# An up projection of a convolved network laid out token-major, with its chunks turned through memory

## The reference, cut to what matters

```
def causal_dwconv(x, w):            # width 3, per channel, over tokens
    ...
def conv_ffn(h, w_up, conv_w, conv_b, w_down):
    u = causal_dwconv(h @ w_up, conv_w) + conv_b      # h 256x1024, w_up 1024x5632
    a, b = jnp.split(u, 2, axis=-1)                   # two halves of 2816
    return (jax.nn.silu(a) * b) @ w_down              # w_down 2816x1024
...
x = x + conv_ffn(rmsnorm(x, norm_ffn[l]), w_up[l], ffn_conv[l], ffn_conv_b[l], w_down[l])
```

## Time and profile before

| | us |
|---|---|
| median of 3 runs | 1137.87 (1137.77 to 1138.19) |
| the profiled execution | 1137.35 |
| its span | 1135.6 |
| TensorE busy | 1126.9 |
| VectorE busy | 755.1 |
| ScalarE busy | 588.0 |
| GpSimd busy | 106.9 |

### The profile page before, as it was taken

How to read it: one execution, slowest core, us unless ns; L and a number is a source line. 1 busy time by engine, 2 the same in 40 slices (tenths; PEclk the granted TensorE clock), 3 DMA queues, 4 the chain that set the end, 5 groups by cost and what they waited for, 6 DMA issues and landing times.

```text
span 1135.6 us, 16361 instructions
## 1 busy us (share of the span) xinstructions
PE 1126.9 (99%) x6345; PEld 984.8 (87%) x6345; DVE 755.1 (66%) x959; ACT 588.0 (52%) x782; POOL 106.9 (9%) x161
## 2 busy tenths in 40 slices
PE   9999999999999999999999999999999999999997
PEld 8998888888889999988888888899888888889886
DVE  6866687657776887853665664665766576655566
ACT  6664654446565766643544443564554365444453
POOL 6410311000011000000000000200500020000020
PEclk9999999999999999999999999999999999999999
DMA  8643753455644765555588766475466568776642
GB/s 259 202 159 98 227 186 115 163 202 180 216 142 132 248 214 186 182 191 183 169 280 258 236 214 205 157 224 164 142 214 216 173 196 283 252 242 223 210 140 77
DMA packets 137294, 220.30 MB, mean 194 GB/s; under 512 B 12565, under 2 KB 70026, under 8 KB 137227
## 3 DMA queue, kind: packets, MB, share of 16 engines
q1 hardware_dynamic: 133625, 209.14, 57.4%
q10 hardware_dynamic: 3506, 10.23, 2.5%
q0 software_dynamic: 96, 0.01, 0.1%
HBM read 212.91 MB, written 6.42 MB: 193 GB/s over the span
## 4 chain that ended last, share of the span: by engine, by line
PE 94%; DVE 3%; DMA 1%; issue 1%; ACT 1%; POOL 0%; POOLq 0%; DVEq 0%; ACTq 0%
PE ACCP L897 28%; PE ACCP L895 28%; PE ACCP L896 28%; PE SMP L1112 3%; DVE CONVF L2338 1%; PE SMP L1105 1%; DVE LO L2209 1%; DMA RAW<-in_w_in_dram 1%; PE SMP L1060 1%; PE SMP L1065 1%; PE SMP L1059 1%; PE SMP L1279 0%; PE SMP L1263 0%; PE SMP L1447 0%; DMA POST_GAIN<-in_ple_post_g_dram 0%
## 5 line engine op out<-in xcount | busy, mean ns | idle before, releaser
L2209 DVE TENSOR_TENSOR LO<-RAW,HI 128x1024 fp32r<-128x1024 f32 x365 | 437.7, 1237 | 210.2 <-ACT HI L1636 205.8
L1636 ACT ACTIVATE HI<-RAW 128x1024 fp32r<-128x1024 f32 x366 | 370.2, 1054 | 262.4 <-PE ACCP L897 214.0
L895 PE MATMUL ACCP<-HI,XH 128*128 128x512 f32 (+1 forms) x712 | 278.0, 391 | 0.0
L897 PE MATMUL ACCP<-HI,XL 128*128 128x512 f32 (+1 forms) x712 | 275.7, 387 | 0.0
L896 PE MATMUL ACCP<-LO,XH 128*128 128x512 f32 (+1 forms) x712 | 275.4, 387 | 0.0
L895 PE MATMUL ACCP<-XH,HI 128*128 128x256 f32 x640 | 181.7, 284 | 0.3 <-DVE CONVF L2338 0.3
L897 PE MATMUL ACCP<-XH,LO 128*128 128x256 f32 x640 | 181.1, 283 | 0.0
L896 PE MATMUL ACCP<-XL,HI 128*128 128x256 f32 x640 | 181.1, 283 | 0.0
L897 PEld LDWEIGHTS ACCP<-HI,XL 128*128 128x128 f32 x712 | 133.7, 188 | 27.3
L896 PEld LDWEIGHTS ACCP<-LO,XH 128*128 128x128 f32 x712 | 133.8, 188 | 26.4
L895 PEld LDWEIGHTS ACCP<-HI,XH 128*128 128x128 f32 x712 | 133.8, 188 | 26.2
(11 more groups left out here) (405 smaller groups left out, 1134.7 us busy)
## 6 DMA issues: line engine op xcount, KB each, us to landing
RAW<-in_w_in_dram SPq DMA_DIRECT2D x104, 512.0 KB, 4.5
RAW<-in_w_up_dram SPq DMA_DIRECT2D x44, 512.0 KB, 4.5
RAW<-in_ffn_w_gate_dram SPq DMA_DIRECT2D x44, 512.0 KB, 4.7
RAW<-in_ffn_w_up_dram SPq DMA_DIRECT2D x44, 512.0 KB, 4.6
RAW<-in_ffn_w_down_dram SPq DMA_DIRECT2D x44, 512.0 KB, 4.3
RAW<-in_w_down_dram SPq DMA_DIRECT2D x22, 512.0 KB, 4.1
scratch_hidden<-TURNED SPq DMA_DIRECT2D x20, 256.0 KB, 5.4
BLOCKS<-scratch_hidden SPq DMA_DIRECT2D x80, 64.0 KB, 2.4
```

Source lines behind the costliest of these rows:

```text
L895: pe.matmul(dst, lhs[0], rhs[0], start=start, stop=False)
L897: return pe.matmul(dst, lhs[1], rhs[0], start=False, stop=stop)
L1636: act.activation(HI[:, n % RING, half_of(half)], RAW[:, n % RAWS, half, :], ACT.Copy).then_inc(hi_ready, 1)
L2209: dve.tensor_tensor(LO[:, s, c], RAW[:, n % RAWS, half, :], HI[:, s, c].bitcast(f32), ALU.subtract).then_inc(lo_ready[s], 1)
```

## The change: what it does

The up projection gets the layout of ffn1 and ffn2. Its first 20 blocks become ten token-major rounds of two blocks (r even: 512 features of half a, r odd: 512 of half b), in five chunks; the last two blocks (256 features of each half) stay feature-major. `f_open`, OPENED and the twelve transposes go. A round's two banks are turned in 32x32 blocks by VectorE straight out of ACCP (`up_turn`), stored to memory in one transfer and read back in four (`up_moves`, placed behind the loads 2r + 7 and 2r + 8). ScalarE then (`up_take`) copies the round to PLAIN and writes the last tap with bias to UA or UB; VectorE adds the two other taps from PLAIN (`chunk_taps`, eight instructions a round). Silu is one instruction of 128x1024 a chunk; the product of a chunk is one GpSimd instruction of 128x1024; the splits HH and HL are one instruction each a chunk. Of the blocks that are prepared behind each chunk's second block, LO's second half is made by GpSimd. The rest tiles keep the old path (`rest_base`, `rest_conv`). The hardware loops of this phase are written out. In ffn1 and ffn2, `hidden_out` becomes one store instead of two and `hidden_in` four reads instead of eight, with both token tiles in each.

```diff
-T_OPEN = {"mix_v": 4, "ple_g": 4, "ffn1": 4, "ffn2": 4}
-F_OPEN = {"up": 3}
+T_OPEN = {"up": 4, "mix_v": 4, "ple_g": 4, "ffn1": 4, "ffn2": 4}
+HALF_ON_POOL = tuple(FIRST["up"] + 4 * c + 1 + RING for c in range(GLU_CHUNKS))
+WIDE = ("up",) + GLUS
-        elif phase in GLUS:
+        elif phase in WIDE:
...
-        UA = at("UA", 44, [P, 2, 2, SEQ])
-        UB = at("UB", 48, [P, 2, 2, SEQ])
+        UA = at("UA", 44, [P, 4, SEQ])
+        UB = [at("UB0", 48, [P, 4, SEQ]), at("UB1", 76, [P, 4, SEQ])]
+        PLAIN = at("PLAIN", 56, [P, 4, SEQ])
+        UP_TURNED = [at(f"UP_TURNED{i}", 60 + 4 * i, [P, 4, NT, 4, 32]) for i in range(2)]
+        UP_BLOCKS = [at(f"UP_BLOCKS{i}", 68 + 4 * i, [P, 4, NT, 4, 32]) for i in range(2)]
+        UP_REST = [at(f"UP_REST{i}", 80 + 2 * i, [P, 2, SEQ]) for i in range(2)]
+        up_rows = [nc.dram_tensor(f"scratch_up{i}", (4, 32, 4, NT * 128), f32) for i in range(2)]
         UAT, UBT = at("UAT", 44, [P, NT, 512]), at("UBT", 48, [P, NT, 512])
-        TURNED, BLOCKS = at("TURNED", 62, [P, NT, 4, 4, 32]), at("BLOCKS", 66, [P, NT, 4, 4, 32])
-        hidden_rows = nc.dram_tensor("scratch_hidden", (NT, 4, 32, 4, 128), f32)
+        TURNED, BLOCKS = at("TURNED", 62, [P, 4, NT, 4, 32]), at("BLOCKS", 66, [P, 4, NT, 4, 32])
+        hidden_rows = nc.dram_tensor("scratch_hidden", (4, 32, 4, NT * 128), f32)
...
-                for m in range(NT):
-                    sp.wait_ge(turned, NT * n + m + 1)
-                    wait(sp, blocks_in, 64 * NT * n)
-                    sp.dma_start(hidden_rows[m].rearrange("b f r c -> (b f) r c"), TURNED[:, m].rearrange("p r k t -> p r (k t)")).then_inc(turned_out, 16)
+                sp.wait_ge(turned, NT * (n + 1))
+                wait(sp, blocks_in, 64 * n)
+                sp.dma_start(hidden_rows[:, :, :, :].rearrange("b f r c -> (b f) (r c)"), TURNED[:, :, :, :, :].rearrange("p r m k t -> p (r m k t)")).then_inc(turned_out, 16)
             def hidden_in(phase, c):
                 n = chunks_before(phase, c)
-                sp.wait_ge(turned_out, 16 * NT * (n + 1))
+                sp.wait_ge(turned_out, 16 * (n + 1))
                 wait(sp, blocks_split, NT * n)
-                for m in range(NT):
-                    for r in range(4):
-                        sp.dma_start(BLOCKS[32 * r:32 * r + 32, m].rearrange("p b k t -> p b (k t)"),
-                                     hidden_rows[m, :, :, r, :].rearrange("b f c -> f b c")).then_inc(blocks_in, 16)
+                for r in range(4):
+                    sp.dma_start(BLOCKS[32 * r:32 * r + 32].rearrange("p b m k t -> p b (m k t)"),
+                                 hidden_rows[:, :, r, :].rearrange("b f c -> f b c")).then_inc(blocks_in, 16)
...
+            def up_moves(loaded):
+                for r in range(2 * GLU_CHUNKS):
+                    if loaded == 2 * r + 7:
+                        for m in range(NT):
+                            acc_is_taken(sp, "up", Turn(r), m)
+                        wait(sp, up_in[r % 2], 64 * (r // 2))
+                        sp.dma_start(up_rows[r % 2][:, :, :, :].rearrange("b f r c -> (b f) (r c)"),
+                                     UP_TURNED[r % 2][:, :, :, :, :].rearrange("p r m k t -> p (r m k t)")).then_inc(up_out[r % 2], 16)
+                    if loaded == 2 * r + 8:
+                        sp.wait_ge(up_out[r % 2], 16 * (r // 2 + 1))
+                        wait(sp, up_base, r - 1)
+                        for q in range(4):
+                            sp.dma_start(UP_BLOCKS[r % 2][32 * q:32 * q + 32].rearrange("p b m k t -> p b (m k t)"),
+                                         up_rows[r % 2][:, :, q, :].rearrange("b f c -> f b c")).then_inc(up_in[r % 2], 16)
+            def load_up():
+                for j in range(GLU_T):
+                    q = j // 2
+                    load("up", Turn(j), t_block(w["w_up"], (q % 2) * DFF + 512 * (q // 2), j % 2))
+                    up_moves(j)
+                for i in range(2):
+                    load("up", Turn(GLU_T + i), f_block(w["w_up"], i * DFF + 512 * GLU_CHUNKS))
+                    up_moves(GLU_T + i)
+                for j in range(COUNT["down"]):
+                    load("down", Turn(j), d_block(w["w_down"], j))
+                    up_moves(GLU_T + 2 + j)
...
-            norm_roots("norm_ffn", "norm_f1")
+            norm_roots("norm_ffn")
+            for c in range(GLU_CHUNKS + 1):
+                if c < GLU_CHUNKS:
+                    n = HALF_ON_POOL[c]
+                    pool.wait_ge(lo_ready[n % RING], 2 * (n // RING) + 1)
+                    lo_half(n, 1)
+                if c:
+                    pool.wait_ge(up_act, c)
+                    pool.wait_ge(up_taps, 2 * c)
+                    y = UB[(c - 1) % 2]
+                    pool.tensor_tensor(y[:, :, :], y[:, :, :], UA[:, :, :], ALU.mult).then_inc(up_gated, 1)
+            norm_roots("norm_f1")
...
+                    if up == "up":
+                        pe.wait_ge(up_lo, k // 4 + 1)
+                    elif k < 4 * GLU_CHUNKS:
                         pe.wait_ge(blocks_split, NT * (chunks_before(up, k // 4) + 1))
-                    elif up in GLUS:
-                        pe.wait_ge(h_lo, FT // 2 + GLUS.index(up) + 1)
                     else:
-                        pe.wait_ge(h_lo, k // 2 + 1)
-                if up in GLUS:
-                    glu(up, r)
-                else:
-                    f_open(up, r)
-                    for j in range(F_OPEN[up], 4):
-                        f_gemm(up, Turn(j), XH, XL)
-                    repeat(pe, 2, FT // 2, 2, step)
+                        pe.wait_ge(h_lo, GLUS.index(up) + 1)
+                glu(up, r)
...
+            pre_gain_load("ffn1_pre_g_2")
+            def up_take(r):
+                act.wait_ge(up_in[r % 2], 64 * (r // 2 + 1))
+                wait(act, up_taps, r)
+                for m in range(NT):
+                    act.activation(PLAIN[:, :, tok(m)].rearrange("p k (b t) -> p k b t", b=4),
+                                   UP_BLOCKS[r % 2][:, :, m].rearrange("p b k t -> p k b t"), ACT.Copy)
+                if r % 2 == 0:
+                    wait(act, up_gated, r // 2)
+                else:
+                    wait(act, up_lo, r // 2 - 1)
+                dst = UB[r // 2 % 2] if r % 2 else UA
+                for i in range(4):
+                    tile = up_tiles(r) + i
+                    ins = act.activation(dst[:, i, :].rearrange("p (m b t) -> p m b t", m=NT, b=4),
+                                         UP_BLOCKS[r % 2][:, :, :, i, :].rearrange("p b m t -> p m b t"), ACT.Identity,
+                                         scale=conv_tap(2, tile), bias=col("ffn_conv_b", tile))
+                ins.then_inc(up_base, 1)
+            def up_silu(c):
+                act.wait_ge(up_taps, 2 * c + 1)
+                act.activation(UA[:, :, :], UA[:, :, :], ACT.Silu).then_inc(up_act, 1)
+            def up_hi_copy(c):
+                act.wait_ge(up_gated, c + 1)
+                copy(HH[:, 4 * c:4 * c + 4, :], UB[c % 2][:, :, :], up_hi)
+            def rest_base(k):
+                b = Turn(GLU_T + k)
+                acc_is_done(act, "up", b)
+                for i in range(2):
+                    tile = k * FT + 4 * GLU_CHUNKS + i
+                    ins = act.activation(UP_REST[k][:, i, :], acc("up", b)[:, i * 256:(i + 1) * 256], ACT.Identity,
+                                         scale=conv_tap(2, tile), bias=col("ffn_conv_b", tile))
+                ins.then_inc(rest_based, 1)
+            for c in range(GLU_CHUNKS):
+                split_ahead("up", Turn(4 * c))
+                if c >= 2:
+                    up_hi_copy(c - 2)
+                if c:
+                    up_take(2 * c - 2)
+                split_ahead("up", Turn(4 * c + 1))
+                if c:
+                    up_silu(c - 1)
+                split_ahead("up", Turn(4 * c + 2))
+                if c:
+                    up_take(2 * c - 1)
+                split_ahead("up", Turn(4 * c + 3))
+            last = GLU_CHUNKS - 1
+            rest_base(0)
+            split_ahead("up", Turn(GLU_T))
+            up_hi_copy(last - 1)
+            up_take(2 * last)
+            rest_base(1)
+            split_ahead("up", Turn(GLU_T + 1))
+            act.wait_ge(rest_taps, 1)
+            act.activation(UP_REST[0][:, :, :], UP_REST[0][:, :, :], ACT.Silu).then_inc(rest_act, 1)
+            up_silu(last)
+            up_take(2 * last + 1)
+            def down_splits(phase):
+                for j in range(COUNT[phase] - RING):
+                    split_ahead(phase, Turn(j))
+                    if j == 1:
+                        up_hi_copy(last)
+                        act.wait_ge(rest_gated, 1)
+                        copy(HH[:, 4 * GLU_CHUNKS:FT, :], UP_REST[1][:, :, :], up_hi)
+            down_splits("down")
...
+                    for half in halves[:1] if n in HALF_ON_POOL else halves:
...
```

(58 more changed lines are left out.)

194 lines of the change are left out of this document (20 added, 174 removed).

## The result

The changed kernel takes **1142.84 us** (median of 6 runs, 1142.08 to 1144.45) against 1137.82 (6 runs, 1137.47 to 1138.70) for the kernel before beside it: ratio 1.0045, 95% interval [1.0035, 1.0056], so 5.0 us slower. The forecast was 1134.6, between 1130.8 and 1140.2. Two versions further down had one of their ten executions each in a slow state (1883 and 2286 us), which is left out of their medians.

What follows compares the result with a forecast made beforehand. TensorE, busy 99% of the span, was taken to bound the kernel. The profiled 1137.35 less 7.6 saved plus 4.3 of delay gave 1134.05, or 1134.6 us on the median, range 1130.8 to 1140.2.

Steps and rivals of the forecast that it cites:

- TensorE's saving: Up projection: with ffn1's list of work it takes 121.2 us instead of 129.5, 7.6 saved after the later start.
- The late start behind XL: Opening of the up projection: the token-major start waits for XL's bank, so TensorE starts 0.6 us late.
- The durations: Up stretch, from the trace: LO half 1.13 us, eight taps 3.15, two transposes 1.22, GpSimd's LO half and product 2.4 each.
- rival 2: VectorE keeps pace, taps quicker from SBUF: cycle 21.8, delay 2.0 or none, 1132.3 to 1130.3 us; chance 0.22.
- VectorE's cycle of 22.3 us: VectorE's work per four-block chunk, with GpSimd's contention, against TensorE's 21.8; with the queue's end TensorE is 4.3 us late.
- the prediction's "only": SBUF contention: only a VectorE instruction with two SBUF inputs contends with a GpSimd one that reads SBUF.
- I take landings as they are: Up's stores and reads keep the trace's landings, store 5.4 us and reads 2.4; slower ones were left to rival 3.
- new stores and reads queue behind loads that were not due: SP's queue in the up stretch: listed under edits that cost nothing, each load being gated by a LO further back.
- the forecast's own signs of being wrong: TensorE waits for LO or banks in the middle of the stretch, or rest_conv(1) ends before TensorE needs it.
- Rival 4: chunk_taps waits for the memory trip ahead of up_turn and LO halves: delay 15.1, 1145.4 us; chance 0.13.
- Rival 3: DMA share rises, landings lengthen about 1 us, each of four cycles 1 us longer: delay 8.3, 1138.6 us; chance 0.20.
- The other edits: SP's order, fewer hidden_out and hidden_in issues in ffn1 and ffn2, unrolled loops, earlier gain row load: cost or gain nothing.

Runs made afterwards that it cites:

- the best version: Changed kernel with the store one load earlier, nothing on GpSimd in this phase, and HL of chunk 3 behind rest_conv(1): 1131.05 us, ratio 0.9945.
- the early store: Changed kernel with each round's store one load earlier in SP's queue, ahead of load 2r+7 instead of behind it: 1135.54 us, ratio 0.9985.
- the half loads: Changed kernel with up's weight loads from the fifth block on bringing half their rows, output not the reference's: 1134.72 us, ratio 0.9975.
- the second run without GpSimd: Changed kernel with the store one load earlier and GpSimd's LO halves and products on VectorE, measured again: 1134.00 us, ratio 0.9961 (first time 1134.12).

## Why the prediction was wrong, by its own steps

**TensorE's saving: right.** In the best version the up projection lasts from 356.2 to 478.2, and 121.6 us without its 0.4 wait for a bank; forecast 121.2. The late start behind XL is 0.5 (355.83 against 355.34); forecast 0.6. So the saving of 7.6 is there (8.3 less 0.6 is 7.7, and 87.0 + 11.5 + 5.4 is 103.9: two slips of 0.1). Without waits and slow clock the early store and the half loads need 121.5 and 121.6 too; the changed kernel needs 1.1 more, and two stops of 0.2 and 0.1 us, at 422.3 and 433.4, too short for the list of waits, are part of that.

**The durations: right, but for one.** Transposes out of PSUM 0.69 long, 0.61 apart, as taken; eight taps 3.25; GpSimd's product 2.39 of 2.4. GpSimd's LO half takes 3.1 on the mean (five), where I had 2.4 from two of them beside VectorE's taps out of PSUM: VectorE's LO halves hold it up as it does them. By the Trainium skill (VectorE: DVE Perf Modes, The TRN2 errata) taps from SBUF would have been shorter; they are not (0.48 us, as from PSUM), so rival 2's first reason falls.

**VectorE's cycle of 22.3 us: close, and not what set the time.** With the trip out of the way, by the early store or by half the loads, turns are 22.0, 22.4 and 21.8 apart, or 22.0, 22.1 and 22.5, VectorE is 95% or more busy from 398 to 464, and TensorE waits at block 21 (2.0 and 1.0; forecast 1.8) and at down's tile 1 (0.6 and 2.2; forecast about 2.5). Those two kernels take 1135.5 and 1134.7; that the first one's sum comes out is in part luck, since its waits are 1.7 short of the forecast's 4.3 and 1.5 of slow clock stand in their place. The contention of two engines in SBUF is shown by VectorE's LO halves of 3.4 us beside GpSimd's against 1.2; the Trainium skill (SBUF — State Buffer, Who interferes with whom) agrees. It names the two-port modes of copies, casts and tensor_scalar as well, which the prediction's "only" leaves out.

**The step that failed is "I take landings as they are".** The forecast had worked out that odd rounds' up_take has 1.3 us in hand, and that the nine rounds bring the traffic to 290 GB/s, above the fullest slice of the page of before, and then used the median landings of ffn1 and ffn2, whose transfers were half as large. Measured in the stretch: store 6.5 instead of 5.4, reads 3.4 with a maximum of 6.1 instead of 2.4 with 3.8: 2.1 us in the medians and 4.9 in the trip of round 7. By the lines above I would put about 1 us of the medians to size (the reads') and about 1 to the stretch (the store's), an estimate from medians of two stretches and not from a run that changes one alone. A landing that stands in a loop with 1.3 us to spare is a term of the sum and not a rival to be priced beside it.

**A second part of the same step:** "new stores and reads queue behind loads that were not due". True of when the data of that load are needed, and not of when the queue gets past it: the load waits for a slot, the slot for a LO half, and that LO half stands behind the very transposes that the store carries. Round 7's store lost 4.1 us there (457.71 to 461.77). One place earlier in the queue gives 7.3 us, one place later costs 64. Of the forecast's own signs of being wrong one came true: TensorE waited for banks in the middle of the stretch, 0.3 us at 444.9 and 1.2 at 457.3.

**Rival 4 was what happened.** It named the place (chunk_taps waiting for the trip through memory, ahead of up_turn), the landings (6.4 and 3.8; medians 6.5 and 3.4) and the price: delay 15.1 and 1145.4. In the profiled execution the delay is 1144.45 - (1137.35 - 7.6) = 14.7: 11.8 of waits at the banks, 1.3 of slow clock behind the long one, the rest placed only in part (above). The slow clock was not in the prediction. That the two delays lie so close is partly luck: on the medians the delay is 12.6 (1142.84 against 1137.82 - 7.6), and the rival reached its 15.1 with landings alone, evenly over four chunks, while in the trace 9.5 of the waiting is at one block, with 4.1 us of queue in the trip ahead of it and GpSimd's hold beside. Rival 3, longer landings that cost 1 us a cycle, had the cause right and stopped half way: it let the loads have 2 us in hand and did not carry the microsecond through store, reads and queue. I gave it 0.20 and rival 4 0.13, though both spoke of the same fact; together they had 0.33 and deserved to lead, since the margin that they attack was the smallest of the whole plan.

**The other edits: about nothing, as forecast.** From the first HH product to the last, over ffn1 and ffn2 with their fewer transfers, the kernel before takes 615.3 us (484.8 to 1100.1) and the changed one 616.4, less the 0.8 at down's tile 1: 0.3 more.

## What to carry to other kernels

When work is moved through memory, write its trip as a loop from one use of the buffer or bank to the next, with the queue's gate in it, and compare the loop with the pace of the engine that it feeds; price the landings at the traffic that the change itself makes, and by what is issued just ahead of them. Where several engines have orders written by hand, find what a queued transfer really waits for: here a store stood behind a load, the load behind a subtraction, and the subtraction behind the producer of the store. An engine that others wait for and that is not busy is not the bound: follow its own waits one step further.

## What the runs showed of the hardware

- A landing goes with the transfers around it and with the size: a store of 512 KB lands in 6.5 us (median) in the up stretch, in 5.6 in ffn1 and ffn2, and in 4.4 when the weight loads are halved (share 0.61 to 0.70 until 464). The share alone does not tell it: with the early store it lands in 4.3 at shares of 0.89 to 0.99, and the reads, now directly behind four halves of loads, in 5.4 instead of 3.4. Reads of 128 KB land in 3.9 in ffn1 and ffn2 where reads of 64 KB took 2.4.
- GpSimd and VectorE hold each other up where both have two inputs in SBUF: VectorE's LO half 3.4 us for 1.2, GpSimd's 3.3 for 2.4, each longer by what the other had still to do.
- TensorE came out of a wait of 9.5 us at a granted clock of 0.50 (1.2 GHz) and stayed there for some 2.9 us more, until 486.5, which cost 1.3 us on top of the wait; behind the waits of 0.3 and 1.2 us the windows show 1.00. Much shorter waits did it too, but not each time: behind 2.03 us in the early store the clock was 0.50 (1.5 us lost), behind 2.56 in the second run without GpSimd 0.51 (1.6 lost), behind 2.02 in the first it stayed at 1.00.
